# Three of the last tile's eight output blocks leave through TensorE and ScalarE, token by token, beside VectorE's five

## What is computed

```python
def _rmsnorm(x, g):
    x32 = x.astype(jnp.float32)
    y = x32 * lax.rsqrt(jnp.mean(x32 * x32, axis=-1, keepdims=True) + EPS)
    return (y * g.astype(jnp.float32)).astype(x.dtype)
...
    merged = jax.nn.sigmoid(m_a) * y_a + jax.nn.sigmoid(m_b) * y_b
    out = x + merged @ w_out
    ...
    y_prompt = _rmsnorm(yp, final_norm_g)
    y_sample = _rmsnorm(ys, final_norm_g)
```

## Time and profile before

| | |
|---|---|
| time, median of 3 runs | 1374.38 us (1374.23 to 1375.24) |
| span of the profiled execution | 1372.1 us |
| PE busy | 1359.5 us, 99% of the span |
| DVE, ACT, POOL busy | 932.0, 685.6 and 198.4 us |

### The profile page before, as it was taken

The page is one execution under the profiler, slowest core; times in us unless marked ns, Lnnn a source line. Parts: engine busy times, 40 slices in busy tenths (PEclk is TensorE's granted clock), DMA queues, the critical chain, the costliest instruction groups (busy, mean ns, idle before and its releaser), DMA issues.

```text
span 1372.1 us, 21266 instructions
## 1 busy us (share of the span) xinstructions
PE 1359.5 (99%) x8272; PEld 1345.2 (98%) x8272; DVE 932.0 (68%) x1642; ACT 685.6 (50%) x992; POOL 198.4 (14%) x200
## 2 busy tenths in 40 slices
PE   9999999999999999999999999999999999999997
PEld 7999999999999999999999999999999999999997
DVE  7899655668975456788844567987445689964443
ACT  6565444355664344556643445665433556653332
POOL 2003021110031211001212110012220200130001
PEclk9999999999999999999999999999999999999999
DMA  6544533246535333465363335653532476534338
GB/s 207 140 131 127 208 122 122 94 130 200 143 108 212 118 123 107 129 193 147 98 222 110 121 110 144 171 156 126 189 122 96 136 170 205 178 108 173 118 100 94
DMA packets 140259, 195.91 MB, mean 143 GB/s; under 512 B 83712, under 2 KB 100480, under 8 KB 138496
## 3 DMA queue, kind: packets, MB, share of 16 engines
q1 hardware_dynamic: 140160, 194.56, 47.1%
HBM read 174.91 MB, written 19.61 MB: 142 GB/s over the span
## 4 chain that ended last, share of the span: by engine, by line
PE 92%; DVE 5%; DMA 1%; issue 1%; ACT 1%; SPq 0%; DVEq 0%; ACTq 0%
PE Z L519 29%; PE Z L521 28%; PE Z L520 28%; DVE wlo L1038 1%; DMA wraw<-w_all 1%; PE B L575 1%; PE B L668 1%; PE B L658 1%; PE B L552 0%; DVE xres L1441 0%; DVE snew L1198 0%; DVE h_b L1078 0%; PE B L519 0%; PE B L521 0%; PE B L520 0%
## 5 line engine op out<-in xcount | busy, mean ns | idle before, releaser
L1038 DVE TENSOR_TENSOR wlo<-wraw,whi 128x1024 fp32r<-128x1024 f32 x280 | 367.0, 1311 | 299.7 <-ACT whi L796 299.5
L519 PE MATMUL Z<-hhi,whi 128*128 128x416 f32 x1576 | 552.7, 351 | 0.0
L520 PE MATMUL Z<-hlo,whi 128*128 128x416 f32 x1576 | 549.4, 349 | 0.0
L521 PE MATMUL Z<-hhi,wlo 128*128 128x416 f32 x1576 | 549.4, 349 | 0.0
L796 ACT ACTIVATE whi<-wraw 128x1024 fp32r<-128x1024 f32 x280 | 295.9, 1057 | 425.2 <-PE Z L521 353.0
L519 PEld LDWEIGHTS Z<-hhi,whi 128*128 128x128 f32 x1576 | 296.0, 188 | 0.9 <-issue 0.6
L520 PEld LDWEIGHTS Z<-hlo,whi 128*128 128x128 f32 x1576 | 296.0, 188 | 0.5
L521 PEld LDWEIGHTS Z<-hhi,wlo 128*128 128x128 f32 x1576 | 295.9, 188 | 0.3
L521 PE MATMUL Z<-mhi,wlo 128*128 128x416 f32 x320 | 112.3, 351 | 0.0
L520 PE MATMUL Z<-mlo,whi 128*128 128x416 f32 x320 | 111.9, 350 | 0.0
L519 PE MATMUL Z<-mhi,whi 128*128 128x416 f32 x320 | 111.5, 348 | 0.0
(11 more groups left out here) (252 smaller groups left out, 1555.2 us busy)
## 6 DMA issues: line engine op xcount, KB each, us to landing
wraw<-w_all SPq DMA_DIRECT2D x280, 512.0 KB, 3.5
xres<-xT SPq DMA_DIRECT2D x5, 1664.0 KB, 7.5
xin<-xT SPq DMA_DIRECT2D x4, 1664.0 KB, 7.8
yT<-xres SPq DMA_DIRECT2D x4, 1664.0 KB, 8.9
v_blocks<-h_vt SPq DMA_DIRECT2D x80, 52.0 KB, 3.1
vtm<-v_blocks SPq DMA_DIRECT2D x20, 192.0 KB, 3.9
ktm<-k_blocks SPq DMA_DIRECT2D x20, 192.0 KB, 3.6
k_blocks<-kt SPq DMA_DIRECT2D x64, 52.0 KB, 1.9
```

Of the source, the lines that this page charges most:

```text
L519: pe.matmul(out, wh, xh, start=first, stop=False)
L520: pe.matmul(out, wh, xl, start=False, stop=False)
L521: return pe.matmul(out, wl, xh, start=False, stop=final)
L1038: dve.tensor_tensor(wlo[n % RING][:], raw(t, n)[:], whi[n % RING][:].bitcast(F32), ALU.subtract).then_inc(wlo_made, 1)
```

## The change

In the last tile alone, blocks 0 to 2 (`TB` = 3) go another way than blocks 3 to 7. After ACT has squared such a block in its unit, ACT also multiplies it in place by its channel weight (`weighted`). The 416 tokens are taken as four groups of 104 (`TC`, `TR`, `TOKENS`). PE transposes each of the three blocks for each group, 12 transposes in all, so that a bank holds 104 tokens as rows and 384 channels as columns (`turn`). DVE adds the last square to the sum of the others (`yall`), and PE multiplies `yall` by two columns of ones, four times, which gives each token's sum in the row of that token. ACT takes Ln and Exp of those 104x4 numbers (`yrc`) and multiplies each bank by its column (`yt`). ACT itself issues two stores into an output array of its own, `yt_out`, each with two token groups. DVE multiplies only blocks 3 to 7 (`output(t, range(TB, KD))`), and SP stores these one block at a time.

```diff
--- before.py
+++ after.py
@@ -109,13 +109,17 @@
 DQ, DG, DR0, DR1, DK, C_FAC = 0, 4, 5, 8, 10, 14
 LOWER, UPPER = slice(0, P // 2), slice(P // 2, P)
 TAIL = [slice(0, T // 2), slice(T // 2, T)]
+TB = 3
+TC = 4
+TR = T // TC
+TOKENS = [slice(c * TR, (c + 1) * TR) for c in range(TC)]
 RC_FIRST = G + 1
 YNORM = 4
 SPLIT_SOONER = [4 * _h + 5 for _h in range(H)]
 OUTPUT_SLOT = (5, 6, 7, 9)
 
 
-def step_kernel(nc, xT, w_all, consts, w_pool, s_in, buf_in, yT, sp_out, pp_out, ss_out, ps_out):
+def step_kernel(nc, xT, w_all, consts, w_pool, s_in, buf_in, yT, yt_out, sp_out, pp_out, ss_out, ps_out):
     with ExitStack() as ctx:
         start = (int(nc.sbuf_base) + 63) // 64 * 64
         top = [start]
@@ -197,6 +201,10 @@
         ysq = [put(f"ysq{i}", [T], F32, r3 + i * B) for i in range(2)]
         yacc = put("yacc", [T], F32, r3 + 6 * B)
         yrs = put("yrs", [T], F32, r3 + 8 * B)
+        yt = put("yt", [TC, TB * P], F32, y_at)
+        assert 4 * TC * TB * P <= 4 * BS
+        yrc = put("yrc", [TC], F32, y_at + 4 * BS)
+        yall = put("yall", [T], F32, y_at + 5 * BS)
         xsq_at = region(2 * B)
         xsq = [put(f"xsq{i}", [T], F32, xsq_at + i * B) for i in range(2)]
         xacc_at = region(B)
@@ -204,7 +212,7 @@
 
         sqh_at = region(B)
         sqh = put("sqh", [T], F32R, sqh_at)
-        sql = {n: put(f"sql_{n}", [T], F32R, at) for n, at in (("head", hg[names.index("osq")]), ("y", r3 + 6 * B))}
+        sql = {n: put(f"sql_{n}", [T], F32R, at) for n, at in (("head", hg[names.index("osq")]), ("y", y_at + 6 * BS))}
         xrs = xsq[0]
 
         xr_at = region(KD * B)
@@ -314,6 +322,8 @@
                                                                sem("split_k"),
                                                       sem("split_v"))
         tail_made, tail_squared, tail_summed = sem("tail_made"), sem("tail_squared"), sem("tail_summed")
+        weighted, turned, yall_made, tokens_summed = sem("weighted"), sem("turned"), sem("yall_made"), sem("tokens_summed")
+        yrc_made, yt_made, yt_stored = sem("yrc_made"), sem("yt_made"), sem("yt_stored")
 
         z_read = [sem(f"z_read{i}") for i in range(NZ)]
         b4_read, b5_read = sem("b4_read"), sem("b5_read")
@@ -452,13 +462,14 @@
                     sp.dma_start(pp_out, ext[:, :, PT:PT + BUF]).then_inc(ends_stored, 16)
                     sp.dma_start(ps_out, exts[:, :, :, NT:NT + BUF]).then_inc(ends_stored, 16)
 
-                    parts = [(0, 2), (2, 4), (4, 6), (6, 7), (7, KD)]
+                    parts = [(j, j + 1) for j in range(TB, KD)]
                     for lo, hi in parts:
-                        sp.wait_ge(y_made, t * KD + hi)
+                        sp.wait_ge(y_made, t * KD + hi - TB)
                         sp.dma_start(yT[t, :, lo:hi, :], xres[:, lo:hi, :]).then_inc(y_stored, 16)
                     sp.wait_ge(ends_stored, 48)
                     sp.wait_ge(snew_stored, 16 * H)
                     sp.wait_ge(y_stored, 16 * (TILES - 1 + len(parts)))
+                    sp.wait_ge(yt_stored, 32)
 
             def values_out(t, h):
 
@@ -638,10 +649,36 @@
                     for bank, c in zip((B5, B6), TAIL):
                         pe.matmul(bank[:, c], ones_r[:], sqh[:, c], start=True, stop=False)
                         pe.matmul(bank[:, c], ones_r[:], sql["y"][:, c], start=False, stop=False)
+                    pe.wait_ge(weighted, TB)
+                    pe.wait_ge(b4_read, b4_done(t, "scores", H - 1))
+                    turn(t, 0, range(TB))
+                    turn(t, 1, range(1))
                     for i, (bank, c) in enumerate(zip((B5, B6), TAIL)):
                         pe.wait_ge(tail_squared, i + 1)
                         pe.matmul(bank[:, c], ones_r[:].bitcast(F32), ysq[(KD - 1) % 2][:, c], start=False,
                                   stop=True).then_inc(tail_summed, 1)
+                    pe.wait_ge(z_sem("out", 6), z_done(t, "out", 6))
+                    for c in range(TC):
+                        if c % 2 == 0:
+                            pe.wait_ge(yall_made, c // 2 + 1)
+                        mm = pe.matmul(z_bank("out", 6)[0:TR, 2 * c:2 * c + 2], yall[:, TOKENS[c]], ones_r[:, 0:2].bitcast(F32),
+                                       start=True, stop=True)
+                    mm.then_inc(tokens_summed, 1)
+                    turn(t, 1, range(1, TB))
+                    for c in range(2, TC):
+                        turn(t, c, range(TB))
+
+            def turn_bank(c):
+                return (B4, B7, z_bank("out", 4), z_bank("out", 5))[c]
+
+            def turn(t, c, blocks):
+
+                if c >= 2:
+                    pe.wait_ge(z_sem("out", c + 2), z_done(t, "out", c + 2))
+                for j in blocks:
+                    mm = pe.transpose(turn_bank(c)[0:TR, j * P:(j + 1) * P], xres[:, j, TOKENS[c]], ident[:])
+                if j == TB - 1:
+                    mm.then_inc(turned, 1)
 
             def sum_squares(bank, what, final=True):
 
@@ -962,6 +999,10 @@
                         h_hi(t + 2, H_SLOT[s])
                     if kind == "out":
                         y_square(t, j)
+                    if kind == "out" and last and j < TB:
+                        act.wait_ge(ysq_made, nth(t, KD, j))
+                        act.activation(xres[:, j, :], xres[:, j, :], ACT.Copy,
+                                       scale=cst[:, C_FG + j:C_FG + j + 1]).then_inc(weighted, 1)
                 if last:
                     act.preload_act_table_set(LN_EXP)
                     for i, c in enumerate(TAIL):
@@ -976,6 +1017,19 @@
                         act.wait_ge(tail_read, i + 1)
                         ins = act.activation(yrs[:, c], yrs[:, c], ACT.Exp, scale=-0.5)
                     ins.then_inc(yrs_made, 1)
+                    act.wait_ge(tokens_summed, 1)
+                    act.activation(yrc[0:TR], z_bank("out", 6)[0:TR, 0:2 * TC:2], ACT.Ln, bias=eps_t[0:TR],
+                                   scale=1.0 / D).then_inc(yrc_made, 1)
+                    act.wait_ge(yrc_made, 1)
+                    act.activation(yrc[0:TR], yrc[0:TR], ACT.Exp, scale=-0.5).then_inc(yrc_made, 1)
+                    act.wait_ge(yrc_made, 2)
+                    for c, bank in enumerate((B4, B7, z_bank("out", 4), z_bank("out", 5))):
+                        act.wait_ge(turned, c + 1)
+                        act.activation(yt[0:TR, c, :], bank[0:TR, 0:TB * P], ACT.Copy,
+                                       scale=yrc[0:TR, c:c + 1]).then_inc(yt_made, 1)
+                        if c % 2:
+                            act.wait_ge(yt_made, c + 1)
+                            act.dma_start(yt_out[:, c - 1:c + 1, :], yt[0:TR, c - 1:c + 1, :]).then_inc(yt_stored, 16)
 
             def y_norm(t):
 
@@ -1400,7 +1454,10 @@
                     for c in TAIL:
                         dve.tensor_tensor(xres[:, KD - 1, c], z_bank("out", KD - 1)[:, c], xres[:, KD - 1, c],
                                           ALU.add).then_inc(tail_made, 1)
-                    output(t, range(KD))
+                    for i, c in enumerate(TAIL):
+                        dve.wait_ge(tail_squared, i + 1)
+                        dve.tensor_tensor(yall[:, c], yacc[:, c], ysq[(KD - 1) % 2][:, c], ALU.add).then_inc(yall_made, 1)
+                    output(t, range(TB, KD))
 
             def y_split(t, last):
 
@@ -1686,7 +1743,7 @@
         "s_in": sh[0].transpose(1, 2, 0, 3), "buf_in": spl[0].reshape(NB, BUF, G, P).transpose(3, 2, 0, 1),
     }
     arrays = {n: np.ascontiguousarray(v) for n, v in arrays.items()}
-    outs = {"yT": x.shape, "sp_out": (P, H, P), "pp_out": (P, G, BUF), "ss_out": (H, P, NB, P),
+    outs = {"yT": x.shape, "yt_out": (TR, TC, TB * P), "sp_out": (P, H, P), "pp_out": (P, G, BUF), "ss_out": (H, P, NB, P),
             "ps_out": (P, G, NB, BUF)}
     nc = bacc.Bacc("TRN2", target_bir_lowering=False, num_devices=1)
     args = [nc.dram_tensor(n, v.shape, mybir.dt.from_np(v.dtype), kind="ExternalInput").ap()
@@ -1694,7 +1751,8 @@
     args += [nc.dram_tensor(n, v, F32, kind="ExternalOutput").ap() for n, v in outs.items()]
     step_kernel(nc, *args)
     r = run_bass_kernel_spmd(nc, [arrays], core_ids=[0]).results[0]
-    y = np.asarray(r["yT"]).transpose(0, 3, 2, 1).reshape(SEQ + SAMPLE, D)
+    y = np.asarray(r["yT"]).transpose(0, 3, 2, 1).reshape(SEQ + SAMPLE, D).copy()
+    y[-T:, 0:TB * P] = np.asarray(r["yt_out"]).transpose(1, 0, 2).reshape(T, TB * P)
     return (
         np.ascontiguousarray(y[:SEQ]).reshape(1, SEQ, D),
         np.ascontiguousarray(y[SEQ:]).reshape(NB, NT, D),
```

## The result

The changed kernel takes 1376.12 us (median of 21 runs, 1375.24 to 1376.5), the kernel before 1374.23 us (21 runs, 1373.25 to 1375.24): ratio 1.0013, 95% interval 1.0007 to 1.0019. It is 1.9 us slower. That is under the 0.2% which the prediction counted as a difference, but the interval excludes no change and the sign that was forecast; the time lies 0.5 us above the range.

A forecast was written before the change was run, and what follows sets the result against it. PE bounds 99% of the span; behind it, DVE and the DMA engines run at one pace. Hidden steps cost 0; the drain gains 0.2 us by flow and up to 0.12 without waits: -0.3, 1374.1 us, range 1372.6 to 1375.6.

The forecast's parts named there:

- The multiplications in place cost 0: ACT's three weight multiplications make block 3's residual about 1.9 us later, hidden by 8 us of cover before PE's unit 7.
- Four transposes ahead of the completing matmuls cost 0: On PE after the last earlier sum: four transposes take 0.44 us, done before 1362.59; 0.5 us if none overlapped.
- ACT's end: ACT's Ln, Exp, four scaled blocks and two issues after the last Exp: second issue at 1367.63, at longest 1368.6.
- First bytes 0.56 us sooner: At the final stores, first block issued at 1365.27, so bytes flow from 1366.07, 0.56 us earlier than before.
- The time outside the span did not grow: Outside the profiled span: 2.3 us expected; growth from a second engine issuing DMAs would make the prediction wrong.
- 13 engines with 8 rows each: Each 104-row `yt_out` store is shared by 13 engines taking 8 rows each, giving 106 small packets in all.
- 16 x 3072 bytes at 24.5: An engine's part of both `yt_out` stores at 24.5 GB/s: 2.01 us, in all 4.89 us, ending at 1370.96.
- since the engines no longer wait for DVE: In the final drain, idle time between stores disappears: up to 0.12 us gained beside 0.2 us by flow.
- C: Final drain: uneven engines (104 rows on 8) or a slow second store, 1.05 us later flow, 1375.4 us; chance 0.2.
- B: The last issue sets the end: engines run faster, last store lands 2.5 us after issue, 1372.8 us; chance 0.15.
- D: No effect: PE's transposes delay `yrs` by 0.5 us and take back the drain's gain, 1374.6 us; chance 0.05.
- Rival A: The drain by the DMA engines sets the end: 0.3 us faster, 1374.1 us, own range 1373.7 to 1374.6; chance 0.6.

The follow-up runs named there:

- f4: The kernel before, with its last tile stored by SP as eight one-block stores instead of five parts: 1373.73 us, ratio 0.9999.
- h1: The changed kernel with token groups of 128, 128, 128 and 32, so ACT's three stores have 128, 128 and 32 rows: 1374.14 us, ratio 0.9998.
- f1: The changed kernel, but SP issues both stores of `yt_out` and ACT none: 1375.38 us, ratio 1.0013.
- g4: The kernel before, with the last tile's first two stores each cut into rows 0 to 103 and 104 to 127: 1376.7 us, ratio 1.002.
- g1: The changed kernel with rows of `yt_out` 6656 bytes apart instead of 6144: 1375.88 us, ratio 1.0014.
- g3: The changed kernel with overlapping token groups of 112 rows and rows of `yt_out` 16384 bytes apart instead of 6144: 1374.91 us, ratio 1.0007.
- h4: The kernel before, with the last tile's first two stores each cut into rows 0 to 63 and 64 to 127: 1376.04 us, ratio 1.0014.
- i2: The kernel before, with the last tile's first two stores each cut into rows 0 to 95 and 96 to 127: 1375.82 us, ratio 1.0011.
- i1: The kernel before, with the last tile's first two stores each cut into rows 0 to 119 and 120 to 127: 1375.92 us, ratio 1.0016.
- i3: The changed kernel with token groups of 128, 128, 128 and 32, its first `yt_out` store cut at row 64: 1374.53 us, ratio 1.0004.

## Why the prediction was wrong

Right, by its steps:

- *The multiplications in place cost 0.* The rows that answer to the earlier trace rows:

```profile
1337.25 0.64 ACT L1004 ACTIVATE xres<-xres,cst 128x416 f32<-128x416 f32 x1
...
1347.96 1.08 DVE L1306 TENSOR_TENSOR xres<-Z,xres 128x416 f32<-128x416 f32 x2
...
1356.91 0.59 DVE L1306 TENSOR_TENSOR xres<-Z,xres 128x416 f32<-128x416 f32 x1 [3.92 <-PE Z L532]
```

The residual of block 3 begins 13.45 us before the last one, where it was 15.38: 1.9 us later, as said, and unit 6's waits for PE as before.

- *Four transposes ahead of the completing matmuls cost 0.* The four took 0.44 us on the chain, and L658 begins 0.84 us behind the residual, as L643 did.
- *ACT's end.* The second issue comes 6.07 us behind the residual, where 5.88 was worked out: the first issue held ACT for 0.62 us, not 0.33. It was hidden.
- *First bytes 0.56 us sooner.* They came at 1365.79, 4.38 us behind the residual instead of 4.92: 0.54 sooner. But this is worth as much without the change (f4).
- *The time outside the span did not grow.* It is 2.2 us in the profiled execution (1375.89 less 1373.7), with a second engine that issues DMAs; 2.3 before.
- *13 engines with 8 rows each.* 106 small packets, 5 x 16 + 2 x 13. By the rule of the Trainium skill that the prediction named ("DMA: Bandwidth & Descriptors", Why a DMA increments its semaphore by 16 and not by 1) it had to be 13, and the trace agrees.

Wrong: the step "16 x 3072 bytes at 24.5" GB/s for each engine. The rate of an engine was read from stores of 128 rows and used for one of 104. The sum had the flow last 4.89 us; it lasted 7.03, while before it lasted 4.62. So 2.4 us more flow less 0.5 us of earlier start are the 1.9 us. A packet of `yt_out` took 183 ns in the mean and up to 569, and those of the same size in a 128-row store took 124 and at most 165: on 16 packets that is 0.94 us on each of the 13 engines. With 40 rows of 1664 bytes at 75 ns, the packets of such an engine come to 5.9 us, 1.0 above the 4.89. The flow was 1.1 us longer than even that, so for so long such an engine had nothing to move; the mean of all 16 was busy for 5.45 of 7.03 us. A plausible link is that SP's last issue stood for 1.87 us while the engines worked off what they had, and that its block, the last to end, started late for it; this was read from the trace, not tested.

One step of the sum was also wrong in itself. The 0.12 us "since the engines no longer wait for DVE" were counted twice: 4.89 us holds no idle time, and the end that it was set against, 1371.16, holds all of it, so these rows gave -0.2 us and not -0.3. By the packets the flow before ended at 1371.30 and lasted 4.62 us, not 4.53, which is as much the other way. Neither moves the forecast by more than 0.14 us.

The rivals: C had the sign and the place ("uneven engines or a slow second store") but not the mechanism: it asked for 8 engines, and its point of decision, 9 rows per engine, was not reached; with 8 rows per engine the time was already worse than its price. Its other branch, a store beside others that lands late, is nearer to what was seen: ACT's second store had its last packet 4.8 us after its issue began, and SP's last store landed 5.7 us after its own. But the slow packets behind that were in no rival. B fell: with 128-row stores the engines were at their limit (362 GB/s at a share of 0.99 in f4), and no stretch moved more than 400. D did not occur: DVE's multiplications begin where they did. Rival A's mechanism, the drain, holds: what sets the end is when bytes start and how fast the engines move them. With stores of 128 rows (h1) A's forecast of 0.3 us under before came out between -0.3 (ratio) and +0.1 us (medians), no measurable difference; in the trace of h1 the bytes end 0.2 us sooner than before.

What stays open is why such packets are slow. Shown is that it needs no second queue (f1, g4), no particular array or row distance (g1, g3, g4), no missing engine (h4, i2) and no lack of 8 rows per engine (i1, and 104 itself). The packets say one thing more: they are not all slow. Of the 208 of `yt_out` in the changed kernel 112 took 115 to 125 ns, like most in h1, and 79 took over 180; in h1 none of 128 did. In the stretches shown of the cuts at 64, 104 and 120 the mean is 258 to 271 ns, about twice the 135 ns of the kernel before. That is what two engines would show that share something which serves one at a time, and it would fit the rate of 206 GB/s at 64 rows, half of 393. No run shows what is shared: it may be a part of SBUF or of the device memory. In common the slow stores have that they do not take all 128 rows at once, so that the engines may be dealt other rows than in a whole store; 8 rows per engine should then have been free of it, unless they are dealt in another order. Which rows an engine takes is in no record here. One store of 32 rows as the last of h1 did no visible harm.

## What to carry to other kernels

Where stores drain at the end of a kernel, count how long the DMA engines work, not when the last store is issued: taking 1.7 us of work from VectorE gave back nothing by itself, since the 0.56 us by which the first bytes start sooner come with a first store of one block, whoever multiplies the rest: f4, with all eight blocks on VectorE, had its last packet 9.12 us behind the residual, and h1, with five, 9.36. Even those 0.56 us were too little to be measured in the time of this kernel. A rate read from stores of all 128 rows is not to be used for others; choose the token groups so that a transposed block fills 128 rows, even if the groups come out unequal (128, 128, 128, 32 instead of 4 x 104 took back the 1.9 us within the scatter). And where a change brings a shape of transfer that no row shows, the range must take in twice its cost (the mean packet took 225 ns instead of 124 in i3), since the busy share alone does not tell a slow engine from a full one.

## What was not expected of the hardware

- Stores of fewer than 128 rows moved 153 to 235 GB/s (64, 104 and 120 rows) and 263 to 276 (96 and 112) with the engines 80 to 100% busy in the stretches shown, where stores of 128 rows move 350 to 400. Cutting two 128-row stores in two, with the same bytes and rows, cost 1.4 to 2.8 us.
- Issues are held up too: SP's took up to 1.87 us (changed kernel) and 1.58 us (cut at 120), against 0.33 to 0.35 before; ACT's first took 0.62 us. With nearly all stores of 128 rows (h1) the longest was 0.82 us, so slow packets lengthen it but are not all of it.
- Two queues with stores of 128 rows at once ran as one does: 4.62 us of flow, 377 GB/s from 1367 to 1371.
